# A hybrid decoder block on one core: x2 stored whole, weight tiles in its spare columns, bf16 one-hots and two spilled units for each block of the gate matrix

## What is computed

```python
z = rmsnorm(h) @ w_in                       # pool channels, q latent, kv latent, rotary key
h = h + concat(pool_mixer(z), attention(z)) @ w_o
# PEER: product-key experts, 8 heads, 16 of 16384 experts each
q = (xn @ wq).reshape(t, 8, 2, 128)         # xn = rmsnorm(h)
sc = einsum('thpc,hpnc->thpn', q, sub_keys) # 128 keys for each half
top_v, top_i = top_k(sc, 16); best of the 16 x 16 sums: top_k(..., 16)
gate = softmax(best_v)                      # expert = i * 128 + j
h = h + sum_k gate * gelu(xn . u[expert]) * v[expert]
h = h + sigmoid(rmsnorm(h) @ w_gate) * (p @ w_proj)
out = rmsnorm(h)
```

## Time and profile before

| | us |
|---|---|
| median of 3 runs | 3168.15 (3166.52 to 3169.14) |
| the profiled execution | 3163.26 |
| its span in the trace | 3161.5 |
| TensorE busy | 3057.4 (97%) |
| VectorE busy | 2492.5 (79%) |
| ACT busy | 1057.1 (33%) |
| POOL busy | 789.8 (25%) |
| DMA read and written | 755.4 MB, 239 GB/s over the span |

### The profile page before, as it was taken

How to read it: one execution, slowest core, us unless ns; L and a number is a source line. 1 busy time by engine, 2 the same in 40 slices (tenths; PEclk the granted TensorE clock), 3 DMA queues, 4 the chain that set the end, 5 groups by cost and what they waited for, 6 DMA issues and landing times.

```text
span 3161.5 us, 46954 instructions
## 1 busy us (share of the span) xinstructions
PE 3057.4 (97%) x17046; PEld 2837.3 (90%) x17046; DVE 2492.5 (79%) x3561; ACT 1057.1 (33%) x1410; POOL 789.8 (25%) x513
## 2 busy tenths in 40 slices
PE   8999999999998889999999999999999999999997
PEld 6777778788887789999999999999999999999775
DVE  7444434499996979999999999999999999976545
ACT  5224423222233543333333333333333333334322
POOL 0120000046665112222222222232323232212000
PEclk9999999999999999999999999999999999999998
DMA  4243222344457679999989999999999999963222
GB/s 161 86 150 116 70 80 93 107 104 114 112 146 265 228 252 357 370 347 339 348 333 347 334 352 342 341 345 340 344 336 347 334 352 343 341 209 107 93 93 93
DMA packets 254900, 756.38 MB, mean 239 GB/s; under 512 B 37232, under 2 KB 90992, under 8 KB 210800
## 3 DMA queue, kind: packets, MB, share of 16 engines
q1 hardware_dynamic: 185328, 414.05, 38.3%
q0 software_dynamic: 64512, 335.64, 28.3%
q10 hardware_dynamic: 4992, 5.80, 0.5%
HBM read 722.28 MB, written 33.10 MB: 239 GB/s over the span
## 4 chain that ended last, share of the span: by engine, by line
PE 79%; DVE 14%; DMA 2%; issue 2%; ACT 1%; SPq 1%; DVEq 0%; ACTq 0%
PE bank L539 24%; PE bank L541 24%; PE bank L540 24%; DVE w_lo L1364 3%; DVE row L1714 1%; DVE one_ij L1742 1%; PE bank L634 1%; PE bank L657 1%; PE bank L635 1%; DMA raw<-in_u_t 1%; DMA raw<-in_v 1%; DVE one_g L1746 1%; DVE x_lo L1906 1%; PE bank L837 1%; DMA row<-in_u_rows,expert 1%
## 5 line engine op out<-in xcount | busy, mean ns | idle before, releaser
L539 PE MATMUL bank<-x_hi,w_hi 128*128 128x352 f32 (+1 forms) x3024 | 1069.3, 354 | 29.0 <-DVE x_lo L1392 10.7
L541 PE MATMUL bank<-x_hi,w_lo 128*128 128x352 f32 (+1 forms) x3024 | 1061.2, 351 | 0.0
L540 PE MATMUL bank<-x_lo,w_hi 128*128 128x352 f32 (+1 forms) x3024 | 1055.2, 349 | 0.0
L539 PE MATMUL bank<-a_hi,w_hi 128*128 128x352 f32 x2048 | 665.4, 325 | 11.6 <-DVE a_lo L1793 6.6
L540 PE MATMUL bank<-a_lo,w_hi 128*128 128x352 f32 x2048 | 664.6, 325 | 0.0
L541 PE MATMUL bank<-a_hi,w_lo 128*128 128x352 f32 x2048 | 664.4, 324 | 0.0
L539 PEld LDWEIGHTS bank<-x_hi,w_hi 128*128 128x128 f32 x3024 | 571.9, 189 | 77.6 <-DVE w_lo L1364 15.3
L541 PEld LDWEIGHTS bank<-x_hi,w_lo 128*128 128x128 f32 x3024 | 571.8, 189 | 43.6
L540 PEld LDWEIGHTS bank<-x_lo,w_hi 128*128 128x128 f32 x3024 | 571.8, 189 | 43.3 <-issue 1.2
L539 PEld LDWEIGHTS bank<-a_hi,w_hi 128*128 128x128 f32 x2048 | 388.0, 189 | 14.3 <-DVE a_lo L1793 7.4
L540 PEld LDWEIGHTS bank<-a_lo,w_hi 128*128 128x128 f32 x2048 | 388.2, 190 | 0.0
(11 more groups left out here) (222 smaller groups left out, 2871.8 us busy)
## 6 DMA issues: line engine op xcount, KB each, us to landing
raw<-in_u_t SPq DMA_DIRECT2D x164, 512.0 KB
raw<-in_v SPq DMA_DIRECT2D x132, 512.0 KB
raw_b<-in_v SPq DMA_DIRECT2D x124, 512.0 KB
raw_b<-in_u_t SPq DMA_DIRECT2D x92, 512.0 KB
g_tile<-gate_matrix SPq DMA_DIRECT2D x32, 704.0 KB, 13.0
raw<-in_w_o SPq DMA_DIRECT2D x32, 512.0 KB
raw<-in_w_q SPq DMA_DIRECT2D x32, 512.0 KB
raw<-in_w_gate SPq DMA_DIRECT2D x32, 512.0 KB
```

What stands on the lines that cost most here:

```text
L539: pe.matmul(out, w_hi[slot][:, blk, :], m_hi, start=first, stop=False)
L540: pe.matmul(out, w_hi[slot][:, blk, :], m_lo, start=False, stop=False)
L541: return pe.matmul(out, w_lo[slot][:, blk, :], m_hi, start=False, stop=last)
```

## The change

- **x2 whole.** `x2_hi` and `x2_lo` become `[P, DC, T]`, 16 chunks of 512 tokens, as x1. The matmuls' moving operand and output are then one run of 512 or 352.
- **Strips and rows.** The columns 352 to 479 of the 16 chunks become a third slot for weight tiles (`place`), which takes the units of slot 0 from unit 76 (`U_SPARE`) to the last group. The old slot 0 (at 8 K and 24 K) becomes the two row buffers. The first row loads wait for the first 76 units; ACT waits for all row work before the last group's first two units; `stage_b` moves into `acc` and into the end of the second `g_blk`, with a wait on SP and one on ACT.
- **bf16 one-hots.** ACT spreads the key numbers and the gate to bf16, each repeated in runs of 4; VectorE splits the gate in three bf16 parts once (`split_gates`). A step compares in bf16 and multiplies three times; TensorE adds three bf16 matmuls for each token. The steps of VectorE stand two ahead of TensorE's, and the early row dots stand one between each.
- **Two units a block.** 8 units stand alone. The first four blocks have two spilled units each, with a step behind each half of a unit (`g_pair`); the last three have one, as before.

```diff
+PAIRS = 4
+PLAIN = ALONE - PAIRS
...
+N_OH = ONE_TB * TB // OH
+RUN = 4
...
-        x2_hi = at("x2_hi", two, [P, NPC, DC, TK], F32R)
-        x2_lo = at("x2_lo", two + 32 * K, [P, NPC, DC, TK], F32R)
+        x2_hi = at("x2_hi", two, [P, DC, T], F32R)
+        x2_lo = at("x2_lo", two + 32 * K, [P, DC, T], F32R)
+        w_hi.append(x2_hi[:, :, TD:TD + P])
+        w_lo.append(x2_lo[:, :, TD:TD + P])
...
-        hk_t = at("hk_t", one, [P, 3, TCD * P])
-        one_ij = [at(f"one_ij{i}", one + (6 + 8 * i) * K, [P, 2, OH, NK]) for i in range(2)]
-        one_g = [at(f"one_g{i}", one + (22 + 4 * i) * K, [P, OH, NK]) for i in range(2)]
+        hk_ij = at("hk_ij", one, [P, N_OH, 2 * OH, RUN], BF16)
+        hk_g = at("hk_g", one + 3584, [P, N_OH, 3 * OH, RUN], BF16)
+        hk_gate = at("hk_gate", one + 8960, [P, N_OH * OH])
+        one_ij = [at(f"one_ij{i}", one + 9856 + 4 * K * i, [P, 2 * OH, NK // RUN, RUN], BF16) for i in range(2)]
+        one_g = [at(f"one_g{i}", one + 9856 + 8 * K + 6 * K * i, [P, 3 * OH, NK // RUN, RUN], BF16) for i in range(2)]
+        iota_b = at("iota_b", one + 9856 + 20 * K, [P, NK // RUN, RUN], BF16)
...
-        stage_b = [at(f"stage_b{i}", two + (22 + 32 * i) * K, [P, 4, P]) for i in range(2)]
+        stage_b = [at("stage_b0", rest + 5 * K, [P, 4, P]), at("stage_b1", one + 60 * K, [P, 4, P])]
...
-        row = [at(f"row{i}", o, [P, D]) for i, o in enumerate((two + 24 * K, two + 56 * K, one + 40 * K - 256, one + 48 * K - 256))]
+        row = [at(f"row{i}", o, [P, D]) for i, o in enumerate((8 * K, 24 * K, one + 40 * K - 256, one + 48 * K - 256))]
...
+        U_SPARE, U_HOME = U_ALONE + 2, peer_unit(N_GROUPS - 1, 0)
+        def place(u, slot, rows=False):
+            if slot == 0 and (U_SPARE <= u < U_HOME if isinstance(u, int) else rows):
+                return 2
+            return slot
...
             for b in range(ONE_TB):
-                if b + ALONE + 2 < U_PEER - U_ALONE:
-                    load_unit(U_BLOCK + b + 2, packed(u_t, spilled(2 * (PH - 1) + ALONE + b + 2)))
+                if b < PAIRS:
+                    load_alone(PLAIN + 2 * b + 2)
+                    load_alone(PLAIN + 2 * b + 3)
                 else:
-                    load_unit(U_BLOCK + b + 2, packed(u_t, U_BLOCK + b + 2 - U_PEER))
+                    load_alone(ALONE + b + 2)
...
+            sp.wait_ge(stage_b_used, 4)
...
             def dense_x2(tensor):
-                return lambda b: tensor[:, 0:TDP, b, :]
...
-                unit(u, slot, tokens(bank[k][:, :]), all_x2(x2_hi), all_x2(x2_lo), **more)
...
             def unit_dense(u, slot, k, **more):
-                unit(u, slot, tokens(bank[k][:, 0:TD]), dense_x2(x2_hi), dense_x2(x2_lo), **more)
+                unit(u, place(u, slot, rows=True), bank[k][:, 0:TD], dense_x2(x2_hi), dense_x2(x2_lo), **more)
...
-                        mm = pe.matmul(out[:, t * P:(t + 1) * P], one_ij[s][:, 1, o, :], one_g[s][:, o, :],
-                                       start=True, stop=True)
+                        for part in range(3):
+                            mm = pe.matmul(out[:, t * P:(t + 1) * P],
+                                           one_ij[s][:, OH + o, :, :].rearrange("p a r -> p (a r)"),
+                                           one_g[s][:, OH * part + o, :, :].rearrange("p a r -> p (a r)"),
+                                           start=part == 0, stop=part == 2)
                     mm.then_inc(g_done, 1)
...
+            def g_pair(b):
+                for j in range(2):
+                    def half_done(quarter):
+                        if quarter % 2:
+                            e = 2 * j + quarter // 2
+                            g_group(b * (TB // OH) + e, e % 2, first=b == 0 and e == 0)
+                    e = PLAIN + 2 * b + j
+                    spill(2 * (PH - 1) + e, e % 2, U_ALONE + e, (U_ALONE + e) % 2, quarter_done=half_done)
...
+                slot = place(u, slot, rows=True)
+                if isinstance(u, int) and U_HOME <= u < U_HOME + 2:
+                    act.wait_ge(row_done, 2 * ALL_ROWS)
...
-                    for i in range(3):
-                        act.wait_ge(hk_turned, i + 1)
-                        act.activation(hk_t[:, i, P:TCD * P], bank[i][:, P:TCD * P], ACT.Copy).then_inc(hk_ready, 1)
+                    def spread(i):
+                        return bank[i][:, P:TD].rearrange("p (q t) -> p q t", t=OH).unsqueeze(3)\
+                            .to_broadcast([P, N_OH, OH, RUN])
+                    act.wait_ge(hk_turned, 3)
+                    act.activation(hk_gate[:, :], bank[2][:, P:TD], ACT.Copy).then_inc(hk_ready, 1)
+                    act.activation(hk_g[:, :, 0:OH, :], spread(2), ACT.Copy).then_inc(hk_ready, 1)
+                    act.activation(iota_b[:, :, :].rearrange("p a r -> p (a r)"), iota[:, :], ACT.Copy).then_inc(hk_ready, 1)
+                    for i in range(2):
+                        act.activation(hk_ij[:, :, OH * i:OH * (i + 1), :], spread(i), ACT.Copy).then_inc(hk_ready, 1)
                     act.wait_ge(topk_step, PER_TOPK * PH)
                     for q in range(4):
...
+            def g_pair(b):
+                s, e = b % 2, PLAIN + 2 * b
+                hi_half(e + 1, 0)
+                g_free(b)
                 g_evict(b, s, 0)
-                hi(b + U_BLOCK + 1, (U_BLOCK + 1 + s) % 2, halves=(0,))
+                hi_half(e + 1, 1)
+                spill_alone(e)
                 g_evict(b, s, 1)
-                hi(b + U_BLOCK + 1, (U_BLOCK + 1 + s) % 2, halves=(1,))
+                hi_half(e + 2, 0)
+                g_evict(b, s, 2)
+                hi_half(e + 2, 1)
...
+                    act.wait_ge(g_stored[1], 16 * (ONE_TB // 2))
+                    rows_stage_b(1)
...
+            def split_gates():
+                def first_of(part):
+                    return hk_g[:, :, OH * part:OH * (part + 1), 0]
+                gates_left = hk_gate[:, :].rearrange("p (q t) -> p q t", t=OH)
+                dve.wait_ge(hk_ready, 2)
+                for part in range(2):
+                    dve.tensor_tensor(gates_left, gates_left, first_of(part), ALU.subtract).then_inc(hk_split, 1)
+                    dve.wait_ge(hk_split, 2 * part + 1)
+                    dve.tensor_copy(hk_g[:, :, OH * (part + 1):OH * (part + 2), :],
+                                    gates_left.unsqueeze(3).to_broadcast([P, N_OH, OH, RUN])).then_inc(hk_split, 1)
+                    dve.wait_ge(hk_split, 2 * part + 2)
...
+            def one_hots(q, s):
+                runs = [P, OH, NK // RUN, RUN]
+                both = [P, 2 * OH, NK // RUN, RUN]
+                if q >= 2:
                     dve.wait_ge(g_done, 2 * q - 2)
-                dve.tensor_tensor(one_ij[s][:, :, :, :], iota[:, None, None, :].to_broadcast(o),
-                                  hk_t[:, 0:2, bass.ds(OH * q + P, OH)].unsqueeze(3).to_broadcast(o), ALU.is_equal)\
-                   .then_inc(oh_ij, 1)
+                dve.tensor_tensor(one_ij[s][:, :, :, :], iota_b[:, None, :, :].to_broadcast(both),
+                                  hk_ij[:, q, :, :].unsqueeze(2).to_broadcast(both), ALU.is_equal).then_inc(oh_ij, 1)
                 dve.wait_ge(oh_ij, q + 1)
-                dve.tensor_tensor(one_g[s][:, :, :], one_ij[s][:, 0, :, :],
-                                  hk_t[:, 2, bass.ds(OH * q + P, OH)].unsqueeze(2).to_broadcast([P, OH, NK]), ALU.mult)\
-                   .then_inc(oh_g, 1)
-            dve.wait_ge(hk_ready, 3)
-            BLOCK_DOT = {1: 13, 2: 14, 4: 15}
-            def g_block(b):
-                for e in range(TB // OH):
-                    one_hots((TB // OH) * b + e, e % 2, first=b == 0 and e < 2)
-                    if e in (1, 2):
-                        lo(b + U_BLOCK + 1, (b + U_BLOCK + 1) % 2, halves=(e - 1,))
-                    if b == 0 and e in (1, 2):
-                        row_dot(10 + e, (10 + e) % 2, row_loads(10 + e))
-                if b in BLOCK_DOT:
-                    k = BLOCK_DOT[b]
-                    row_dot(k, k % 2, row_loads(k))
-            for b in range(ONE_TB):
-                g_block(b)
+                for part in range(3):
+                    ins = dve.tensor_tensor(one_g[s][:, OH * part:OH * (part + 1), :, :], one_ij[s][:, 0:OH, :, :],
+                                            hk_g[:, q, OH * part:OH * (part + 1), :].unsqueeze(2).to_broadcast(runs),
+                                            ALU.mult)
+                ins.then_inc(oh_g, 1)
+            dve.wait_ge(hk_ready, 5)
+            def lo_half_of(e, half):
+                lo(U_ALONE + e, (U_ALONE + e) % 2, halves=(half,))
+            one_hots(0, 0)
+            one_hots(1, 1)
+            for q in range(N_OH):
+                b, e = divmod(q, TB // OH)
+                if b < PAIRS:
+                    lo_half_of(PLAIN + 2 * b + 1 + e // 2, e % 2)
+                elif e < 2:
+                    lo_half_of(ALONE + b + 1, e)
```

(79 more changed lines are left out.)

39 lines of the change are left out of this document (19 added, 20 removed).

## The result

The changed kernel takes 3119.56 us (median of 4 runs, 3118.16 to 3121.09), the kernel before beside it 3167.34 (4 runs, 3164.73 to 3169.14): a ratio of 0.9854, 95% interval 0.9841 to 0.9866, 47.8 us faster. I had said 3121.0. The profiled execution of after took 3120.19 us, its span 3118.4.

What follows compares the result with a forecast made beforehand. Expert groups, half the span, were taken as bound by TensorE's matmul rate. 28 + 11.7 + 7.5 = 47 us took the profiled 3163.26 to 3116; with 4.9 us to the median, 3121. Range 3112 to 3128; 8 in 10, 3101 to 3158.

Steps and rivals of the forecast that it cites:

- Gate product: Gate product at the end: whole x2 saves 9.8 ns on each of 768 matmuls, 7.5 us, all on the path.
- Expert groups: Groups 1 to 30, paced by TensorE: whole x2 saves 0.39 us a group, 11.7 us in all.
- so I cost the runs at nothing: Weight tiles in the strips: VectorE's writes in shorter runs cost nothing; otherwise its slack of 3.7 us a group covers it.
- Query heads: Seven query heads: TensorE saves 8.5 us, but VectorE is slower (41.1 against 40.3 us), so it turns into waits.
- The 0.9 us ahead of them: The two units ahead of the first query head: whole x2 saves 96 x 9.8 ns, 0.9 us, which counts.
- One-hots: One-hot steps on VectorE: bf16 at two elements a cycle, 3.3 us a step, saving 0.2 us a step.
- the first rival: bf16 one-hots run at one element a cycle: 2.7 us more a step, 75 us over 28, 3196 us; chance 0.08.
- TensorE's one-hot matmuls: One-hot steps on TensorE: 24 bf16 matmuls of 128 columns at 70 ns each, 1.7 us a step, as before.
- The third rival: TensorE (106 ns a matmul) or DMA (7.5 us a step) paces the pairs: 3130 to 3134 us; chance 0.17.
- Two units a block: Gate-matrix blocks: one-hots start about 973, steps of 6.8 us, end about 1121 for 1149.96; 28 us with the 0.9.
- New waits: Added waits cost nothing, `stage_b` 1 at most 1.3 us; rival, a large new wait: 3151 us, chance 0.05.

Runs made afterwards that it cites:

- experiment 10: The changed kernel itself, unaltered, run again as the base beside experiment 9 on the same chip: 3119.40 us, ratio 0.9871.
- Experiment 3: The changed kernel with the high and low halves of the strip weight tile exchanged between x2_hi and x2_lo: 3121.87 us, ratio 0.9856.
- experiment 5: The changed kernel with the strip tile 32 columns further right (columns 384 to 511, byte 1536 of the row): 3113.74 us.
- experiment 9: The kernel of experiment 5 (strip tile in columns 384 to 511), timed over 5 runs: 3112.82 us, ratio 0.9845.
- Experiment 7: The kernel of experiment 2 (x2 in pieces) with half of the top-16 candidates left out in each query head: 3130.70 us.
- Experiment 8: The changed kernel (x2 whole) with half of the top-16 candidates left out in each query head: 3109.23 us.
- Experiment 2: The kernel before with only the bf16 one-hots and two units a block; x2 in pieces, weight tiles and row buffers as before: 3137.34 us, ratio 0.9908.
- Experiment 11: The changed kernel with 12 units alone and one unit a block (PAIRS = 0), bf16 one-hots and layout kept: 3145.27 us, ratio 0.9945.
- experiment 6: The changed kernel with no tile in the strips from group 2 on and two row buffers in place of four: 3417.22 us, ratio 1.0807.

## Why the prediction was right, and where it was not

**The time** was 1.4 us off, and that close it is luck: two errors of 4 and 5.5 us cancel in it. Between the profiled executions the gain is 43.1 us and not 47. And I carried the 4.9 us by which the profiled execution of before lay below its median over to after, whose profiled execution lies 0.6 above; in experiment 10 it lies 3.9 below. There is no fixed offset to carry. The gain itself is known to a few us only: 47.8 by the medians here, 42.9 by those of experiment 10 (3162.28 and 3119.40).

**Gate product:** 7.5 us said, 7.2 measured. Spacing (3059.87 - 2941.98)/520 = 0.2267 us.

**Expert groups:** the one step whose mechanism was wrong. I had 0.39 us a group, 11.7 in all; the groups gave 0.23, 7.0 in all. The step that failed is "so I cost the runs at nothing": I priced the strips for VectorE and ACT, which write them, and not for TensorE, which reads its weights there. In the steady groups a unit with x2 moving and its tile at byte 1408 of the row takes 0.3 us more than with the tile in its own place, more even than the pieces had cost (7.89). Experiment 3 excludes the 32 KB as the cause, and experiments 5 and 9 show that moving the tile by 128 bytes removes the cost. How it arises stays open: the place alone does not decide it, as the last section shows. The base of my price was too high as well: I took `a`, 0.1617, as the pace of whole operands; x2 whole runs at 0.1611 (experiment 9), so with a well placed tile a group would gain 0.47 us.

**Query heads:** the 8.5 us came to nothing, as said, and `cell` is written every (862.94 - 698.72)/4 = 41.06 us. TensorE is busy 195.36 of the 200 us from 700 on, where it was 199.82. Experiments 7 and 8 show that the gain existed (6.9 us over seven heads, 8.5 priced) and that VectorE hid it. The 0.9 us ahead of them, which I had kept, can't be told from these traces: 0.6 at the first head, nothing at the last, with 1.6 us between two executions of one kernel.

**One-hots:** double rate as taken, and the first rival is refuted as a forecast and confirmed as a mechanism: with runs of 1 it would have come true at 3184 us (3196 said). The row of the Trainium skill (VectorE: DVE Perf Modes, The perf-mode tier table), 1224 ns, agrees with 1218; runs of 1 keep its bf16 type and take 2283.

**TensorE's one-hot matmuls:** I said 70 ns. From 1120.14 to 1121.47, 24 of them take 1.33 us, 55 ns each; the eight fp32 ones of a step before took 1.70 us. The Trainium skill's figure of about 81 ns (TensorE: Matmul & The Clock Gate, Back-to-back issue gap) does not hold in this stream; the measurement decides. The third rival's two conditions, 106 ns and 7.5 us a step by DMA, did not come about as a pace: the DMA engines moved 279 GB/s over the stretch. Late rows do account for the two long steps, 7.5 and 7.1 us, in which VectorE waited 1.05 and 0.6 us for a row load.

**Two units a block:** said 973 to 978, 1066, 1073, blocks of 15.8, 1121. The rows have the one-hots from 973.66, the step-by-step loop from 979.79, its thirteenth step over at 1065, and 1121.47. Blocks 4 to 6 are 15.8 us apart (their third comparison at 1081.20, 1096.99 and 1112.74). The size of a step was off, 6.41 for 6.8, because I added lengths and not starts; two steps of 7.5 and 7.1 us and a start 2 us later took that back. Experiment 2 gives 29.4 us for the part where 28 stood. The agreement of 28.3 us with the 28 is luck to some us: in experiment 10 the same kernel begins its scaled products 4.5 us earlier. Experiment 11 shows that it takes the pairs and the early start, which fill VectorE's idle time from 960 on. I had not split them from the cheaper one-hots, and no run has pairs beside float32 one-hots. By an estimate these would bring most of it: from start to start, comparison and products take VectorE 3.06 us in bf16 (973.66 to 976.72) and took 3.46 in float32 (1015.56 to 1019.02), so 28 steps would be some 11 us longer, of 29.4.

**New waits:** `stage_b` 1 is written at 1124.75 in 1.28 us, ahead of a gelu that waits for VectorE's scaling; nothing, as said. No wait that the layout adds shows otherwise. What four row buffers are worth I had not priced; experiment 6 does.

## What to carry to other kernels

When a tile moves in memory, price it for every engine that reads it, and in the engine that binds the stage first: a tile that costs its writers nothing took back, through TensorE, two fifths of what I had priced in the groups. A gain on one engine of a coupled stage is worth the other's slack and no more, so compare both periods before adding it. To overlap work, ask first who is idle beside it: the same cheaper one-hots, with the same row dots between them, brought nothing after twelve units and, started four units earlier beside pairs of units, 26 us.

## What the runs showed of the hardware that was not expected

- A weight tile that starts at byte 1408 of rows of 2048 costs 0.0061 us a matmul in the steady groups when the moving operand is x2 in the same rows (0.1665 against 0.1604 in its own place). At byte 1536 strip and own place both take 0.1611. Exchanging the halves between two regions of 32 KB changes nothing. With `a` moving, the misplaced tile takes 0.1617, the spacing of all `a` matmuls before.
- Byte 1408 alone does not decide. Of the 49 units with x2 and a strip tile that run without a break after 890 us in the changed kernel, 44 have 0.166 or 0.167 and 5 have 0.158, less than in the tile's own place; at byte 1536 (experiment 9) all have 0.160 or 0.161. One unit in the blocks has both, before and after the one-hot matmuls in its middle, with the same tile and operands:

```profile
972.82 0.33 PE L551 MATMUL bank<-x_lo,x_hi 128*128 128x352 f32 x1
...
976.31 0.32 PE L552 MATMUL bank<-x_hi,x_lo 128*128 128x352 f32 x1
...
978.43 0.33 PE L551 MATMUL bank<-x_lo,x_hi 128*128 128x352 f32 x1
...
982.10 0.32 PE L552 MATMUL bank<-x_hi,x_lo 128*128 128x352 f32 x1
```

  (976.31 - 972.82)/22 = 0.1586 us, then (982.10 - 978.43)/22 = 0.1668. What makes a unit take one pace or the other was not found, nor whether the distance from the moving operand or the tile's own alignment matters.
- bf16 operations of two inputs on VectorE take the double rate when the innermost run of both has 2 or 4 elements side by side (687 ns for 1024), and the single rate when one is repeated by a stride of 0 (1224). A broadcast costs a table of twice the size and not four times.
- 24 bf16 matmuls of 128 columns, each with its own weights, run at 55 ns at the granted clock 1.00.
- Executions of one kernel differ by 4 to 5 us around the one-hots and the first three groups: the changed kernel began its scaled products at 1156.32 in one profile and at 1151.84 in another, with spans of 3118.4 and 3113.8 us.
